# A planner's distances between DVE roots and the PE work that takes them, and mixed values split pair by pair

## What is computed

```python
def first_block(x, mem, ...):
    h = rms_norm(x, g_mix)
    q, k, v, z, xbc, dt_raw = split(h @ w_in)
    attn = rms_norm(dilated_attention(q, k, v, positions, g_q, g_k), g_attn_out)
    ssm = ssd_mixer(z, xbc, dt_raw, ...)        # conv, silu, chunked scan, gate,
                                                # rms_norm in 4 groups of 256
    x = x + concatenate([attn, ssm]) @ w_out
    x = x + cross_attention(rms_norm(x, g_cross), rms_norm(mem, g_mem), ...)
    return x + square(relu(rms_norm(x, g_mlp) @ w_up)) @ w_down

def hybrid_layer(x, ...):
    xr, gr, q, k, v, qi, ki, wi, g_rnn, g_att = split(x @ w_in)
    y_rnn = rg_lru(causal_dwconv(xr), ...) * gelu(gr)
    y_att = dsa_attention(rope(q), rope(k), v, rope(qi), rope(ki), wi, topk=64)
    merged = sigmoid(g_rnn) * y_rnn + sigmoid(g_att) * y_att
    x = layer_norm(ALPHA * x + merged @ w_out)
    f = (silu(gate) * up) @ w_down              # gate, up = split(causal_dwconv(x @ w_up))
    return layer_norm(ALPHA * x + f)
```

## Time and profile before

| | us |
|---|---|
| median of 3 runs | 2687.77 |
| lowest, highest | 2686.26, 2689.82 |
| the profiled execution, its own time | 2687.87 |
| its span, first to last instruction | 2686.1 |
| PE busy | 2642.1 (98%) |
| DVE busy | 1783.1 (66%) |
| ACT busy | 1336.9 (50%) |
| GpSimd busy | 94.6 (4%) |
| DMA | 485 MB, 56.8% of 16 engines |

### The profile page before, as it was taken

How to read it: one execution, slowest core, us unless ns; L and a number is a source line. 1 busy time by engine, 2 the same in 40 slices (tenths; PEclk the granted TensorE clock), 3 DMA queues, 4 the chain that set the end, 5 groups by cost and what they waited for, 6 DMA issues and landing times.

```text
span 2686.1 us, 52776 instructions
## 1 busy us (share of the span) xinstructions
PE 2642.1 (98%) x22462; PEld 2591.5 (96%) x22462; DVE 1783.1 (66%) x2630; ACT 1336.9 (50%) x1817; POOL 94.6 (4%) x64
## 2 busy tenths in 40 slices
PE   8999999999999999999999999999999999999997
PEld 8998899899999999999899999999999999999997
DVE  6787779675555555565687786556676656665666
ACT  5574566454344443444445774444465435543553
POOL 2000021010000000000000000000200000000002
PEclk9999999999999999999999999999999999999998
DMA  6544545466666665565554556665466666666662
GB/s 241 182 150 142 173 150 190 146 205 192 194 196 193 194 196 192 194 195 176 167 168 153 173 185 193 196 194 167 142 196 193 195 194 196 192 194 196 194 192 95
DMA packets 136603, 488.45 MB, mean 182 GB/s; under 512 B 15152, under 2 KB 17584, under 8 KB 136368
## 3 DMA queue, kind: packets, MB, share of 16 engines
q1 hardware_dynamic: 136368, 485.09, 56.8%
HBM read 482.93 MB, written 2.10 MB: 181 GB/s over the span
## 4 chain that ended last, share of the span: by engine, by line
PE 92%; DVE 6%; ACT 1%; issue 1%; DMA 0%; SPq 0%; ACTq 0%; DVEq 0%
PE ps L797 91%; DVE WL L1763 2%; DVE XL L1771 1%; PE ps L800 1%; DVE T L1771 1%; DVE xT L1763 1%; DMA cst<-in_cst 0%; ACT P L1248 0%; ACT WH L1248 0%; DVE P L1767 0%; DVE T L1763 0%; DVE P L2048 0%; DVE small L1771 0%; DVE AL L1771 0%; ACT L1248 0%
## 5 line engine op out<-in xcount | busy, mean ns | idle before, releaser
L1763 DVE TENSOR_TENSOR WL<-raw,WH 128x1024 fp32r<-128x1024 f32 x907 | 1124.0, 1242 | 754.8 <-ACT WH L1248 754.6
L1248 ACT ACTIVATE WH<-raw 128x1024 fp32r<-128x1024 f32 x907 | 961.7, 1061 | 1283.8 <-PE ps L797 1282.0
L797 PE MATMUL ps<-XH,WH 128*128 128x256 f32 x5024 | 1402.5, 279 | 20.6 <-DVE WL L1763 11.3
L797 PE MATMUL ps<-XL,WH 128*128 128x256 f32 x5024 | 1390.8, 277 | 0.0
L797 PE MATMUL ps<-XH,WL 128*128 128x256 f32 x5024 | 1390.6, 277 | 0.0
L797 PEld LDWEIGHTS ps<-XH,WH 128*128 128x128 f32 x5024 | 944.4, 188 | 27.4 <-issue 18.9
L797 PEld LDWEIGHTS ps<-XL,WH 128*128 128x128 f32 x5024 | 944.5, 188 | 2.3 <-issue 1.5
L797 PEld LDWEIGHTS ps<-XH,WL 128*128 128x128 f32 x5024 | 944.2, 188 | 0.3
L797 PE MATMUL ps<-AH,WH 128*128 128x256 f32 x1856 | 513.1, 276 | 0.6 <-DVE AL L1763 0.4
L797 PE MATMUL ps<-AL,WH 128*128 128x256 f32 x1856 | 512.3, 276 | 0.0
L797 PE MATMUL ps<-AH,WL 128*128 128x256 f32 x1856 | 512.3, 276 | 0.0
(11 more groups left out here) (229 smaller groups left out, 1567.2 us busy)
## 6 DMA issues: line engine op xcount, KB each, us to landing
raw<-in_w_up SPq DMA_DIRECT2D x304, 512.0 KB, 3.7
raw<-in_w_in SPq DMA_DIRECT2D x224, 512.0 KB, 3.5
raw<-in_w_down SPq DMA_DIRECT2D x216, 512.0 KB, 3.6
raw<-in_w_out SPq DMA_DIRECT2D x64, 512.0 KB, 3.5
raw<-in_w_gates SPq DMA_DIRECT2D x64, 512.0 KB, 3.5
raw<-in_w_ckv SPq DMA_DIRECT2D x16, 512.0 KB, 3.3
raw<-in_w_cq SPq DMA_DIRECT2D x8, 512.0 KB, 4.2
raw<-in_w_co SPq DMA_DIRECT2D x8, 512.0 KB, 3.3
```

Of the source, the lines that this page charges most:

```text
L797: return e.matmul(out, l, r, start=start, stop=True, skip_group_check=True)
L1248: return e.activation(out, x, func, **kw)
L1763: return e.tensor_tensor(out, a, b, op)
```

## The change

1. `norm_spread` is no longer in `ON_PE`: it stands one slot after `norm_rs` (and `norm_row` one later still).
2. `chain` takes `apart`: steps named there stand a slot after the one ahead. `head_steps` uses it for `sm_tr` of units 4 to 7.
3. The chain of the group norm `ssm` starts 2 slots later: `t + 4` for `t + 2`.
4. `mg_hi`/`mg_lo` of pairs 0 to 5 are planned from the slot after their granule of `att 3`, and `mg_hi` waits for that granule alone.
5. In ACT's order within a slot `qk_sq` comes ahead of `sm_exp`.

```diff
-ON_PE = {"norm_sum", "norm_spread", "dt_rows", ...
+ON_PE = {"norm_sum", "dt_rows", ...
...
-    def chain(self, t, unit, steps, *bufs):
+    def chain(self, t, unit, steps, *bufs, apart=()):
...
-            off.append(off[-1] + (two not in ON_PE or one in ON_PE))
+            off.append(off[-1] + (two not in ON_PE or one in ON_PE or two in apart))
...
-    return P.chain(t, u, steps, *bufs)
+    return P.chain(t, u, steps, *bufs, apart=("sm_tr",) if 4 <= u < 8 else ())
...
-            ssm = P.chain(t + 2, u // 2, ("ssm_sq", "ssm_sum", "ssm_rs", "ssm_spread", "ssm_gain"),
+            ssm = P.chain(t + 4, u // 2, ("ssm_sq", "ssm_sum", "ssm_rs", "ssm_spread", "ssm_gain"),
...
-        P.chain(max([s for s, x in P.due["at_mul"].items() if u in x][0], E("att", 3)) + 1, u, ("mg_hi", "mg_lo"))
+        P.chain(max([s for s, x in P.due["at_mul"].items() if u in x][0], P.slot[P.first["att", 3] + u]) + 1, u,
+                ("mg_hi", "mg_lo"))
...
             def mg_hi(u):
-                on.wait_ge(s["gemm"], P.count("att", 3))
+                on.wait_ge(s["gemm"], P.first["att", 3] + u + 1)
...
                 for u in P("sm_copy", t):
                     sm_copy(u)
+                for u in P("qk_sq", t):
+                    qk_sq(u)
                 for u in P("sm_exp", t):
                     sm_exp(u)
...
                 for u in P("qk_wide", t):
                     qk_wide(u)
-                for u in P("qk_sq", t):
-                    qk_sq(u)
```

More of the change, by code:

```diff
@@ L121 @@
 GELU_WAIT = (4, 4, 2, 2, 0, 0, 0, 0)
-ON_PE = {"norm_sum", "norm_spread", "dt_rows", "dt_sums", "cb_pe", "xs_pe", "ssd_spread", "ssd_y", "ssm_sum",
+ON_PE = {"norm_sum", "dt_rows", "dt_sums", "cb_pe", "xs_pe", "ssd_spread", "ssd_y", "ssm_sum",
          "ssm_spread", "qk_sum", "qk_spread", "qk_rot", "sm_qk", "sm_tr", "sm_av", "hn_sum", "hn_spread", "qi_rot",
```

## The result

The changed kernel takes 2673.41 us in the median of four executions (2672.46 to 2677.66), the kernel before 2687.74 (2686.26 to 2689.82, four): ratio 0.9948, interval 0.9936 to 0.9960, so 14.0 us less, between 10.8 and 17.2. Forecast were 10.6 us less, 2677.3, in a range of 2674.5 to 2683.5. The direction is right; the time lies 1.1 us under the range. Two later comparisons of the same kernel gave 2674.67 (0.9948) and 2675.59 (0.9954).

A forecast was written before the change was run, and what follows sets the result against it. PE, busy 98% of the span, bounds the kernel, so only its waits can be won: 4.96 + 1.8 + 0.95 + 1.55 + 1.3 = 10.6 us, giving 2677.3 us, range 2674.5 to 2683.5 with rivals.

The forecast's parts named there:

- the spreads: Norms 1 and 2, slot 113: two roots hidden behind two granules, 1.3 us won; delaying norm 0 costs 0.
- The split: Start of `w_out2`: pairs split six slots early remove PE's wait, 3.28 us, and the half-clock granule behind, 1.68; 4.96 us.
- slow granule: Granule behind the wait at `w_out2` took 4.40 us instead of 2.72, partly at 1.2 GHz; 1.68 us to win.
- The rival in which the half clock stays: Granule behind the `w_out2` wait stays slow, or the clock falls elsewhere: 1.68 us less won, 2679.0; chance 10%.
- The group norm: Scan's group norm two slots later: waits at `qk_sum` 1 and a mask go, 1.73 + 0.5 − 0.4 = 1.8 us.
- both new waits: DVE's queue makes PE wait about 0.2 us at `ssd_y` 7, slot 62, and 0.2 at `ssm_spread` 3, slot 67.
- the rival in which the waits move on by a root: DVE queues miss by a root (2.2 us); only split and square remain, 5.9 us won, 2682.0; chance 15%.
- The squares: `qk_sq` 4 ahead of four exponentials on ACT: PE's wait of 0.8 and 0.17 go, 0.95 us won.
- The transposes: Softmax scalings ahead of `sm_tr` hidden behind one more granule: 1.2 us in two waits, twice 0.17; 1.55 us won.
- the slower rival: Slot 113's two roots don't fit DVE's idle time; 17.9 us lost in the full stretch against 10.6 won, 2695; chance 5%.
- PE busy time down by about 1.7 only: Sign of a right forecast: PE's busy time falls about 1.7 us, the rest of the gain coming from its idle time.

The follow-up runs named there:

- the split alone: Kernel before with only the mg_hi/mg_lo splits planned pair by pair ahead of `w_out2`: 2682.67 us, ratio 0.9979 (0.9970 to 0.9988).

## Why the prediction was wrong, point by point

Two steps failed. The prediction **took the low clock of TensorE as a fixed price of one place**, read from one execution: 1.68 us at slot 621 and nothing anywhere else. The runs show it behind the wait at slot 59 too, in 7 of 8 traces, worth 1.4 us on average. (Besides, norm 3 was left out of the spreads, 0.41 us of idle time.) And it **took the spread from three runs**, 3.6 us, where executions of one kernel lie 11 us apart. The mechanisms of the five edits held; the last 1.1 us below the range is luck of the executions, as two repeats lie inside it.

**The split.** Right: 3.28 us of wait and 1.68 of slow granule, 4.96 forecast and found. The rival in which the half clock stays fell: in none of the nine traces without the open wait is slot 621 slow, and with the split alone no granule of slots 622 to 640 is slow in its place. But 1.68 was the price of one execution; 7 of 9 have it, and over these nine slot 621 is 1.2 us longer than 2.72 on average.

**The group norm.** 1.8 forecast, 1.82 found, with both new waits where the queue on DVE put them: 0.30 at `ssd_y` 7 in slot 62 (forecast 0.2), and 0.14 at `ssm_spread` 3 in slot 67 (forecast 0.2), so the rival in which the waits move on by a root fell. Here **a term was left out**: the low clock behind the wait of 1.56 us. The trace before had none at slots 59 to 62, and I took that as how it always is. In 7 of 8 traces with that wait it costs 1.6 us: 1.4 us more for this edit on average.

**The squares.** 0.95 forecast, 1.03 found.

**The transposes.** 1.55 forecast, 1.73 found. The scalings still meet an addition on GpSimd, with the same price as in rows 6, and nobody waits for them, as a granule lies between:

```profile
363.77 1.01 DVE L1768 TENSOR_SCALAR P<-P,small 128x128 f32<-128x128 f32 x4
...
365.00 2.07 DVE L1768 TENSOR_SCALAR P<-P,small 128x128 f32<-128x128 f32 x4
...
365.42 1.29 POOL L1724 TENSOR_TENSOR T<-T 128x512 f32<-128x512 f32 x1 [3.59 <-ACT T L1249]
```

**The spreads.** 1.3 forecast, 1.35 found for norms 1 and 2; none lost in slots 16 to 21 nor in the full stretch, so the slower rival fell. Norm 3, which I left out, gives 0.41: its wait was only 0.12 us long, but slot 135 took 3.33 us with it and 2.86 without, so a slow restart behind it came on top.

**The sum.** The removed idle time is 3.28 + 1.82 + 1.03 + 1.73 + 1.35 + 0.41 = 9.6 us, where my terms without the clock made 8.9. The clock behind the two waits is worth 1.6 × 7/8 + 1.6 × 7/9 = 2.6 us on average, an estimate from 8 and 9 traces, where I had 1.68 at one place. Together 12.3 us, which lies in the interval of each of the three comparisons (ratios 0.9948, 0.9948 and 0.9954, or 14.0, 14.0 and 12.4 us), and puts the changed kernel at 2675.4, inside the range. Of the 3.4 us by which the first comparison exceeds the forecast, 1.7 are so accounted for; the rest is within what executions of one kernel differ by.

**The range** was too narrow. I took the spread of executions from three runs, 3.6 us. The 98 executions of the kernel before in the comparisons here, on four chips, reach from 2682.9 to 2693.9, and on one of these chips alone they lie 9.5 us apart. It goes with the clock: the mean span is 2681.1 us at a mean clock of 0.996, 2685.2 at 0.994 and 2691.8 at 0.991. The first trace of the changed kernel, its fastest of four executions, fell on a good one: its slot 1 is among 2 of 18 that were not slow. Its two repeats, 2674.67 and 2675.59, lie inside the range. "PE busy time down by about 1.7 only" was wrong for the same reason: it fell by 7.8, with 1.68 of it at slot 621, 1.6 at slot 1 and 3.3 from slot 622 to the end of the layer norm.

## What to carry to other kernels

A wait on TensorE can cost more than its length: here 1.6 us behind waits of 1.6 and of 3.1 us, in most traces but not in all. One trace doesn't tell whether a place has it, so read the granted clock behind each wait in two or three traces of the same kernel before pricing it, and take the run-to-run range from the clock. To say what an edit won, compare the starts of the slots on both sides of its place; differences where nothing was edited are not its own. And where idle matmuls in a wait kept the clock up (one trace shows it at slot 620), removing the wait gave that and the wait's length besides.

## What the runs showed of the hardware

The clock level behind a wait differed between executions of one and the same kernel: 1.00 and 0.83 over the same 10 us, behind waits of 1.56 and of 3.1 us. Which of the two came went with the point of the clock's beat at which the stretch began, in the layer norm without exception in 18 traces: slot 622 starts at 0.20 to 0.36 of a beat in one sort and at 0.77 to 0.16 in the other. Removing either wait kept the clock at 1.00 at points where an open wait had lost it. With six idle matmuls into an unused PSUM bank in the wait of 3.1 us the clock was 1.00 at such a point too (one trace), but eight of them instead of three in the layer norm, where the wait is 2.9 us long and 128x1 sums run ahead, changed nothing. At the kernel's start, where PE stands 1.3 to 3.8 us for the constants' DMA, 16 of 18 traces had a slow second granule (4.0 to 5.3 us instead of 2.84 or 2.88), and 11 us between the fastest and the slowest execution of one kernel go with a mean clock between 0.996 and 0.991. What in the layer norm brings the low clock, its waits or its 128x1 sums, was not found.
